# A hybrid decoder layer on one core: the steps of two token blocks are set to later slots of one streamed gather loop

## What is computed

```python
def _layer(x, mem_k, mem_v, lru_buf, h0, sc_buf, lp):
    m, nb, nh, ns = _mixer(x, mem_k, mem_v, lru_buf, h0, sc_buf, lp)
    x = _layernorm(DEEPNORM_ALPHA * x + m, lp['ln1_g'], lp['ln1_b'])
    f = _peer(x, lp['peer_wq'], lp['peer_keys'], lp['peer_u'], lp['peer_v'])
    x = _layernorm(DEEPNORM_ALPHA * x + f, lp['ln2_g'], lp['ln2_b'])

# _mixer: proj = x @ w_in (1024 -> 2048 columns), split in three groups
#   A: causal conv of width 4, gates r and i (block-diagonal matmuls, sigmoid), linear scan, times gelu(gate)
#   B: y = B * conv3(C * x);  C: softmax attention of 4 heads over 256 memory tokens
#   RMS norm of each group, then y @ w_out

def block(xb):                                    # _peer, 128 tokens at a time
    qb = jnp.einsum('td,de->te', xb, wq).reshape(PEER_BLOCK, PEER_HEADS, 2, PEER_DK // 2)
    sk = jnp.einsum('thpd,hpkd->thpk', qb, keys).astype(jnp.float32)
    v1, i1 = lax.top_k(sk[:, :, 0], PEER_TOPK)
    v2, i2 = lax.top_k(sk[:, :, 1], PEER_TOPK)
    ...
    g = jax.nn.softmax(top_s, axis=-1).astype(xb.dtype)
    act = jax.nn.gelu(jnp.einsum('td,thkd->thk', xb, u_tab[e]), approximate=False)
    return jnp.einsum('thk,thkd->td', g * act, v_tab[e])
```

## Time and profile before

| what | value |
|---|---|
| time, median of 3 runs | 3114.4 us (3113.41 to 3116.53) |
| the profiled execution | 3113.92 us, of which 3112.1 us are the span from the first to the last instruction |
| busy PE / DVE / ACT / POOL | 80% / 69% / 43% / 41% of the span |
| bytes moved | 1236.40 MB, a mean of 397 GB/s |
| mean granted TensorE clock | 0.860 |
| slots 80 to 298 (second block) | about 415 us to 1010 us |
| slots 368 to 660 (third block) | about 1213 us to 2020 us |

### The profile page before, as it was taken

How to read it: one execution, slowest core, us unless ns; L and a number is a source line. 1 busy time by engine, 2 the same in 40 slices (tenths; PEclk the granted TensorE clock), 3 DMA queues, 4 the chain that set the end, 5 groups by cost and what they waited for, 6 DMA issues and landing times. The chain is left out here.

```text
span 3112.1 us, 35134 instructions
## 1 busy us (share of the span) xinstructions
PE 2504.1 (80%) x10252; PEld 734.7 (24%) x10252; DVE 2146.2 (69%) x4925; ACT 1323.0 (43%) x4059; POOL 1273.2 (41%) x1092
## 2 busy tenths in 40 slices
PE   9989988898887997878867879876676666666776
PEld 5633322222221332223322223311111111110010
DVE  3676779888756477887776686676667666764554
ACT  2354455555435343554543353343333333333333
POOL 0034443444444444444444444444444444444443
PEclk9999999999997998999989879966776677777666
DMA  5489999999999999999999999999999999999997
GB/s 218 135 316 384 411 419 410 378 412 420 420 420 418 420 420 420 412 403 399 419 420 415 420 391 420 420 422 421 421 420 412 416 421 415 418 417 422 416 413 319
DMA packets 184150, 1236.40 MB, mean 397 GB/s; under 512 B 21011, under 2 KB 21267, under 8 KB 44179
## 3 DMA queue, kind: packets, MB, share of 16 engines
q0 software_dynamic: 156672, 1140.92, 89.0%
q1 hardware_dynamic: 27062, 92.58, 7.8%
q10 hardware_dynamic: 224, 0.66, 0.1%
HBM read 1226.91 MB, written 7.17 MB: 397 GB/s over the span
## 5 line engine op out<-in xcount | busy, mean ns | idle before, releaser
L731 POOL DMA_INDIRECT arena<-in_uv,idxT x1088 | 1273.0, 1170 | 1813.7 <-PE ps L1056 1570.2
L1742 DVE CUSTOM_DVE_ANT_0 arena<-arena 128x1024 f32<-128x1024 f32 x1088 | 1327.6, 1224 | 788.5 <-DMA arena<-in_uv,idxT 718.2
L1056 PE MATMUL ps<-arena,wset 128*32 128x512 f32 x4352 | 1372.3, 737 | 578.9 <-ACT wset L1306 570.1
L1301 ACT ACTIVATE gel<-acts 128x1 f32<-128x1 f32 x1088 | 219.0, 201 | 1427.1 <-DVE acts L1742 1422.1
L1056 PEld LDWEIGHTS ps<-arena,wset 128*32 128x32 f32 x4352 | 175.4, 118 | 1484.3 <-ACT wset L1306 1283.9
L1306 ACT ACTIVATE wset<-gated,gel 128x32 f32<-128x32 f32 x1088 | 349.6, 321 | 90.5 <-ACT gel L1301 1.8
L1299 ACT ACTIVATE gated<-arena,gT 128x32 f32<-128x32 f32 x1088 | 334.5, 307 | 0.1
L758 PE MATMUL ps<-arena 128*128 128x384 f32 (+1 forms) x768 | 306.5, 520 | 6.8 <-DMA arena<-in_w_in 6.8
L942 PE MATMUL ps<-arena 128*128 128x384 f32 (+3 forms) x896 | 287.3, 449 | 0.7 <-DVE small L1505 0.7
L1038 PE MATMUL ps<-arena 32*128 32x512 f32 x704 | 241.9, 769 | 1.3 <-ACT arena L1277 0.9
L942 PEld LDWEIGHTS ps<-arena 128*128 128x128 f32 x896 | 146.1, 190 | 199.0 <-issue 153.4
(11 more groups left out here) (189 smaller groups left out, 1555.6 us busy)
## 6 DMA issues: line engine op xcount, KB each, us to landing
arena<-in_wq SPq DMA_DIRECT2D x56, 512.0 KB
arena<-in_w_in SPq DMA_DIRECT2D x47, 512.0 KB
arena<-in_uv,idxT POOLq DMA_INDIRECT x1088
arena<-in_w_outs SPq DMA_DIRECT2D x24, 512.0 KB, 8.5
arena<-in_xT SPq DMA_DIRECT2D x4, 768.0 KB, 9.5
out_y<-arena SPq DMA_DIRECT2D x17, 128.0 KB
arena<-in_wkv SPq DMA_DIRECT2D x1, 2048.0 KB, 15.3
scratch_x<-arena SPq DMA_DIRECT2D x4, 512.0 KB, 3.3
```

Of the source, the lines that this page charges most:

```text
L731: pool.indirect_dma_start(out=ring[n % RING], out_offset=None, in_=A["uv"], in_offset=bass.IndirectOffsetOnAxis(ap=idxT[t % 2][:, col:col ...
L1056: last = mm(ps[r0:r0 + 32, hf * HALF:(hf + 1) * HALF], wset[n % SETS][:, :], v[:, hf * HALF:(hf + 1) * HALF], start=first, stop=final)
L1301: A_(gel[:, n % COLS:n % COLS + 1], acts[:, n % COLS:n % COLS + 1], ACT.Gelu).then_inc(gelus, 1)
L1742: V.tensor_tensor_reduce(out=ring[n % RING][:, 0:D], in0=ring[n % RING][:, 0:D], in1=xrep[g % 2], scale=1.0, scalar=0.0, op0=ALU.mult, op1 ...
```

## The change

In the second and third blocks most steps of ACT and DVE are put one to three slots later against the PE steps that they read. The projections' copies move from 6 to 8 slots after their `half`, for the first 14 of 16. The gate steps of the first three of four channels move by one to three slots (`late`), the conv by one. In the attention, `mx`, `ex`, `nz`, `at`, `tc`, `av` and `ty` move by one or two slots, and in the second block the rounds after the first begin two slots later as a whole. `z`, `xe` and `we` move by one, `q2` by three, `sh` by one, and the four `lb` of the second norm are spread wider. In the windows of 32 slots `copy_idx` and `copy_gates` stand one slot later. The projections (`half` and its second part), `gr` and `gi`, the output projection and the queries on PE stay where they were. The orders of SP and POOL are as before. No computation and no transfer is added or taken away.

```diff
     for i, (name, c) in enumerate(PROJ[b]):
         put("pe", o + 8 * i, b, "half", (name, c))
         put("pe", o + 8 * i + 4, b, name, c)
-        put("act", o + 8 * i + (6 if i < 14 else 7), b, name, c)
+        put("act", o + 8 * i + (8 if i < 14 else 7), b, name, c)
     for c in range(CL):
         x = o + 16 + 24 * c
-        put("dve", x + 9, b, "cv", c)
+        late = 1 if c < CL - 1 else 0
+        put("dve", x + 9 + late, b, "cv", c)
         put("pe", x + 15, b, "gr", c)
-        put("act", x + 15, b, "sr", c)
+        put("act", x + 16 + late, b, "sr", c)
         put("pe", x + 15, b, "gi", c)
-        put("act", x + 15, b, "si", c)
-        put("act", x + 16, b, "ta", c)
...
     def attend(r, x):
-        put("dve", x + 1, b, "mx", r)
-        put("act", x + 2, b, "ex", r)
-        put("dve", x + 3, b, "nz", r)
-        put("pe", x + 5, b, "at", r)
-        put("act", x + 6, b, "tc", r)
+        put("dve", x + 2, b, "mx", r)
+        put("act", x + 3, b, "ex", r)
+        put("dve", x + 5, b, "nz", r)
+        put("pe", x + 6, b, "at", r)
+        put("act", x + 8, b, "tc", r)
 
     for r in range(ROUNDS[b]):
-        x = o + 18 + 16 * r
+        x = o + 18 + 16 * r + (2 if b == 1 and r else 0)
         put("pe", x, b, "as", r)
         attend(r, x)
-        put("pe", x + 8, b, "av", r)
-        put("dve", x + 9, b, "ty", r)
+        put("pe", x + 9, b, "av", r)
+        put("dve", x + 11, b, "ty", r)
...
+    def idx_step(u):
+        return sel_step(u) + (2 if per(u) == 1 else 1)
...
-                if at == sel_step(u) + 1:
+                if at == idx_step(u):
                     copy_idx(u)
```

More of the change, by code:

```diff
@@ L139, in plan_later_block @@
         put("pe", o + 8 * i + 4, b, name, c)
-        put("act", o + 8 * i + (6 if i < 14 else 7), b, name, c)
+        put("act", o + 8 * i + (8 if i < 14 else 7), b, name, c)
     for c in range(CL):
         x = o + 16 + 24 * c
-        put("dve", x + 9, b, "cv", c)
+        late = 1 if c < CL - 1 else 0
+        put("dve", x + 9 + late, b, "cv", c)
         put("pe", x + 15, b, "gr", c)
-        put("act", x + 15, b, "sr", c)
+        put("act", x + 16 + late, b, "sr", c)
         put("pe", x + 15, b, "gi", c)
-        put("act", x + 15, b, "si", c)
-        put("act", x + 16, b, "ta", c)
-        put("dve", x + 18, b, "ra", c)
-        put("dve", x + 20, b, "rc", c)
-        put("act", x + 23, b, "sd", c)
-        put("dve", x + 25, b, "re", c)
-    put("dve", o + 89, b, "sh", 0)
+        put("act", x + 16 + late, b, "si", c)
+        put("act", x + 17 + late, b, "ta", c)
+        put("dve", x + 18 + 2 * late, b, "ra", c)
+        put("dve", x + 20 + 2 * late, b, "rc", c)
+        put("act", x + 23 + 2 * late, b, "sd", c)
+        put("dve", x + 25 + 3 * late, b, "re", c)
+    put("dve", o + 90, b, "sh", 0)
     put("dve", o + 128, b, "sh", 1)
     def attend(r, x):
-        put("dve", x + 1, b, "mx", r)
-        put("act", x + 2, b, "ex", r)
-        put("dve", x + 3, b, "nz", r)
-        put("pe", x + 5, b, "at", r)
-        put("act", x + 6, b, "tc", r)
+        put("dve", x + 2, b, "mx", r)
[3 more added lines that the diff above has]
+        put("act", x + 8, b, "tc", r)
     for r in range(ROUNDS[b]):
-        x = o + 18 + 16 * r
+        x = o + 18 + 16 * r + (2 if b == 1 and r else 0)
         put("pe", x, b, "as", r)
         attend(r, x)
-        put("pe", x + 8, b, "av", r)
-        put("dve", x + 9, b, "ty", r)
+        put("pe", x + 9, b, "av", r)
+        put("dve", x + 11, b, "ty", r)
     x = o + 140
     if b == 2:
-        put("dve", o + 15, b, "q2")
+        put("dve", o + 18, b, "q2")
         for i in range(4):
@@ L189, in plan_later_block @@
         for ti in range(3):
-            put("act", x + 28 * half + 24, b, "z", (ti, half))
+            put("act", x + 28 * half + 25, b, "z", (ti, half))
     x += 56
@@ L196, in plan_later_block @@
         for i in range(4):
-            at = o + 29 + (0, 2.5, 16, 18.5)[i]
+            at = o + (30, 33, 48, 64)[i]
             put("pe", at, b, "lb", (2, i))
-            put("act", int(at) + 1, b, "lb", (2, i))
+            put("act", at + 2, b, "lb", (2, i))
     for ti in range(3):
@@ L215, in plan_queries @@
         put("pe", x + each * side, b, "wq", side)
-        put("act", x + each * (side + 1), b, "we", side)
+        put("act", x + each * (side + 1) + (1 if b else 0), b, "we", side)
 FIRST_PE = """
@@ L1313, in _ @@
                     softmax_exp(u)
-                if at == sel_step(u) + 2:
+                if at == idx_step(u) + 1:
                     copy_gates(u)
```

2 lines of the change are left out of this document (1 added, 1 removed).

## The result

The changed kernel took 3125.1 us (median, 3123.95 to 3127.55), the kernel before, on the same chip, 3114.4 us (3110.48 to 3116.53): a ratio of 1.0034 with a 95% interval of 1.0023 to 1.0044. It is slower by 10.7 us, above the range of the prediction. The profiled execution took 3123.95 us, with a span of 3122.0.

The account below looks back on a forecast made before the run. Transfers near 420 GB/s were taken as the bound, with 10.9 us of idle DMA time to win. 3113.9 - 5.5 + 1.5 = 3109.9 us for the profiled execution, so 3110.4 us median; range 3103 to 3121.

Parts of the forecast that it names:

- The ceiling: Idle time of the DMA engines at five places in the second and third blocks: 10.9 us, the most the change can win.
- The gains: Four terms for closing idle DMA time in the second and third blocks: 5.5 us together, between 0 and 9.7.
- That at 610: Second block, 610 to 620 us: moved steps shorten DVE's wait for `mx`; 2.0 us won, bounds 0 and 3.5.
- that at 1400: Third block, 1400 to 1420 us: `mx` and `ty` stand two slots behind PE; 2.0 us won, bounds 0 and 2.6.
- 520 to 580: Second block: DVE nearly full, its work spread but not shortened; 1.0 us won, bounds 0 and 1.8.
- 1830: 1830 to 1850 us: later `xe` and `we` may win 0.5 of 1.8 us of idle DMA time.
- 1780 to 1800: PE late by its half clock and its steps not moved: 0 of 1.2 us won.
- the price of the forward waits: PE's `gi` and next `half` wait for ACT copies a slot later: 0.75 us at slots 111 and 135, 1.5 in all.
- Rival B: Forward waits at `gi` and next `half` on PE become the bound: +10 us, 2 of gains left, 3122.4 us; chance 0.13.
- Rival D: PE's new waits drop its clock in six of eight places: +10 us less 4 of gains, 3120.4 us; chance 0.06.
- The sentence on the table loads: ACT: a load takes only its 1.28 us row; by the skill's 2.66 us, slots 119 to 122 would cost more.
- wrong for the costs: Signs: DMA share below 0.9 around 500 to 590 us, or new low-clock stretches right behind the forward waits.

Follow-up runs that it names:

- gates_only: The kernel before with only the change's later projection copies, gate steps and `q2`, attention and all else as before: 3123.9 us, ratio 1.0028 to before.
- combined: Changed kernel, second block's attention rounds 2 and 5 unshifted, third block's `lg`, `sr`, `si` at old slots, `mx` ahead of its slot's gate arithmetic: 3113.2 us.
- combined_plus7: Changed kernel, second block's rounds 2 and 5 unshifted, `mx` ahead of gate arithmetic, `lg` of channels 0 to 2 at 7 slots, `sr`, `si` one slot earlier: 3112.7 us.
- candidate: Changed kernel with `lg`, `sr`, `si` at old slots, second block's rounds unshifted, `mx` ahead of gate arithmetic, second `lb` one slot earlier: 3119.3 us.
- combined_tail: combined with `z`, `xe` and `we` one slot earlier, as in the kernel before: 3111.7 us, ratio 0.9990 to before.
- busy_wait: Changed kernel with `gr` run nine times instead of once in three places ahead of PE's stand, same values written: 3118.7 us, ratio 1.0008 to before.
- mx_first: Changed kernel with `mx` a tenth of a slot earlier in DVE's list, ahead of the gate arithmetic: 3122.7 us, ratio 1.0029 to before.

## Why the prediction was wrong

**The ceiling** was right. The loss and the gain both lie in idle time of the DMA engines, and the sum of 10.8 us accounts for the result.

**The gains** were right in size in two places, and not shown in their cause. That at 610 was 3.5 us (taken 2.0) and that at 1400 2.6 us (taken 2.0), both at their upper bound. The prediction lays both to shorter waits of DVE for `mx` and `ty`. In the third block these waits did go. At slot 150 the wait for `mx` is 4.0 us in after, longer than the 2.7 us of before, and yet the hole is gone. gates_only has the attention's steps and the `lb` as before, and its share is 1.01 from 610 to 620 and 1.00 from 1400 to 1420. In combined, combined_plus7 and candidate, where at most 0.6 us of the hole at slots 401 to 407 is left, 1.6 to 2.0 us stand again between 1400 and 1420, without a wait for `mx` or `ty` there in combined. A hole may go just because another, earlier one has let the engines catch up. Against that, combined is full at 610 with 1.0 us ahead of it, and combined_tail at 1400 too. So the cause is open, and that the two sizes fit is in part luck.

Two of the four terms had the wrong sign: 520 to 580 lost 1.8 us (taken +1.0), and 1830 lost 1.2 us (taken +0.5). The bounds of both ended at 0 and should have reached below. Together the four give +3.1 us where 5.5 were taken; 1780 to 1800 moved to 1800 to 1810 and is 1.0 us for 1.2. The forecast's lower bound was also summed wrong: gains of 9.7 for 5.5 and a cost of -1.6 for +1.5 make -7.3 us, not -5.8. That changes nothing of the result, which lies on the other side.

**The step that failed is the price of the forward waits**: 1.5 us were taken, within -1.6 and 5, and 14.1 us were measured (4.6 + 5.0 + 4.5). That step had four parts.
- The mechanism was right: `gi` waits for an `lg` that stands a slot ahead, and the combines and POOL are queued behind it.
- The stand was priced at 1.4 us where DVE lags and 3.9 us at the gathers' pace, from ACT's mean pace. What is left of the three long stands without the exponential is in that range (3.1, 3.9 and 2.2 us by the estimate above), and at the other five places PE stood 2.52, 2.15 and 1.07 us and twice not at all. What was missed is what else stands in ACT's list between the point of the wait and its target: `ex` with two loads in slots 135 and 183, and the exponential of the lookups in slot 400. Only three of the eight places have such a thing, and these three lost 14 us. The loads' 1.28 us was among the rows; the position of `ex` was in the order of the changed kernel, and the text looked at slot 111, where nothing stands between.
- Of the places charged, 111 and 135, the first cost nothing that shows and the second 4.6 us. Slots 183 and 399 were held to have slack.
- Rival B decided from where the lag passes the slack "in two places or more", with 2.5 us each at four places. It named the outcome (3122.4, measured 3125.1) and got 0.13. Its price of 2.5 us was half of what a real place cost; two of its four places (135 and 183) were real, and the third real one lies in the third block.

**Rival D was the other half.** Behind the three stands the clock was 0.50 for 10 to 14 us each, and keeping PE busy gave back 6.4 us. The objection raised against it, that the clock fell many times in before without a hole, holds for stretches such as 1776 to 1797 us, with a clock of 0.50 and a share of 0.99; behind the three stands the share was 0.57 to 0.69 at the same clock. It needed three places and not six. B and D aren't rivals but one chain, and their joint chance should have been far above 0.19. The Trainium skill (TensorE: Matmul & The Clock Gate, Part 1), with its sentence on the throttled default state, agrees with the 0.50 behind each stand and with the 1.00 of busy_wait.

**A wait that was missed**: ACT's, for an `mx` that DVE comes to a slot later. The change puts `mx` and `ex` one slot apart in the table, but DVE's pieces ahead of `mx` push it one slot on. It made the hole at slot 121, 3.7 us of idle time, which mx_first takes away.

**The sentence on the table loads** spoke of slots 119 to 122, where 5 loads now stand for 4. Each load took 1.28 us there again; their number grew by one in these slots, and the hole there went with mx_first, which leaves the loads where they are.

**What would show it**: the share at 610 and 1400, and the waits for `mx`, were as written (the third block's wait for `mx` is gone; at slots 134, 150 and 182 they were 3.2, 4.0 and 5.0 us, above the 1 to 3 given). The idle times of PE before the second L798 were 5.91, 6.00 and 5.08 us at slots 135, 183 and 399, above the 1.4 to 3.9 given, 2.52 and 2.15 us at 423 and 447, within it, 1.07 us at 159, and none at 111 and 471. The idle time of the DMA engines was 21.7 us, outside the 5 to 9 with which the forecast stands or falls. Both signs for "wrong for the costs" came true.

**What stays open**: what closed the holes at 610 and 1400 us; why candidate has a hole at slot 122 without any forward wait; and the idle time at slots 576 to 591, 1.4 us in gates_only and 2.9 to 6.7 in the other kernels.

## What to carry to other kernels

Where a step on one in-order engine waits for a step that stands later in another engine's loop, list every instruction that the other engine has between the two, table loads included: that list comes on top of the slots' own pace, and another part of the same change may have lengthened it. Then add the time in which TensorE catches up at half clock behind a stand, if the trace shows such stretches. Before a hole that is gone is booked as a gain, look for one that came ahead of it. Distances written in a table hold only between steps that run where they are put; a list that works in pieces pushes them on, so distances are to be read from the order.

## What the hardware showed that was not expected

- Work of no use on PE was a gain: 24 matmul calls more (5.43 us of repeated L800 in the first place) and 6.4 us less, since the granted clock stayed at 1.00 in the three stretches in which it was 0.50.
- A wait of POOL of 10.58 us in after comes from a stand of PE of little more than half that length: 5.91 us of standing, then 2.08 + 1.92 us for work that takes 1.13 + 1.05 at full clock.
- A copy with a gelu pays for its neighbour: `lg` at 1312.89 loaded a table of 1.28 us, as the lookups' exponential had come in between.
